# Attention probabilities scaled on GpSimd instead of VectorE, with a ring of factor columns between them

## What is computed

```python
def masked_softmax(s, ok):
    s = jnp.where(ok, s, NEG)
    m = jnp.max(s, -1, keepdims=True)
    e = jnp.where(ok, jnp.exp(s - m), 0.0)
    return e / jnp.maximum(jnp.sum(e, -1, keepdims=True), TINY)
```

```python
    o_att = (gate[..., 0:1] * o_cmp + gate[..., 1:2] * o_slc + gate[..., 2:3] * o_swa).reshape(B, T, D_ATT)
```

## Time and profile before

| | |
|---|---|
| time, median of 3 runs | 2127.87 us (2126.4 to 2128.36) |
| the profiled execution's time | 2130.53 us |
| its span, first to last instruction | 2129.0 us |
| attention, layer 0 | from 204.7 to 394.4 us, 189.7 us |
| attention, layer 1 | from 1102.2 to 1285.8 us, 183.6 us |
| busy share of the span | PE 89%, DVE 53%, ACT 37%, POOL 3% |
| granted TensorE clock, mean of the span | 0.945 of full speed |

### The profile page before, as it was taken

How to read it: one execution, slowest core, us unless ns; L and a number is a source line. 1 busy time by engine, 2 the same in 40 slices (tenths; PEclk the granted TensorE clock), 3 DMA queues, 4 the chain that set the end, 5 groups by cost and what they waited for, 6 DMA issues and landing times.

```text
span 2129.0 us, 25885 instructions
## 1 busy us (share of the span) xinstructions
PE 1901.0 (89%) x9617; PEld 1475.5 (69%) x9617; DVE 1121.8 (53%) x1984; ACT 778.5 (37%) x1110; POOL 69.0 (3%) x80
## 2 busy tenths in 40 slices
PE   6999789979999999989988899749999999999970
PEld 4777555769999999967765558536666666666650
DVE  2684567444544544437746663335555555555546
ACT  3012455332121121130135452345555555555531
POOL 0000000000000000000000000020000000000003
PEclk9999799999999999999999899859999999999995
DMA  6331001011222222053210000158888888888863
GB/s 237 119 96 60 21 20 40 30 50 60 80 80 80 92 85 82 21 168 117 69 60 20 31 30 26 79 202 327 347 345 346 348 346 346 345 347 342 348 276 125
DMA packets 69404, 332.29 MB, mean 156 GB/s; under 512 B 15682, under 2 KB 28802, under 8 KB 50562
## 3 DMA queue, kind: packets, MB, share of 16 engines
q1 hardware_dynamic: 60498, 303.11, 37.9%
q0 software_dynamic: 7088, 24.43, 3.2%
q10 hardware_dynamic: 1728, 3.54, 0.4%
HBM read 312.26 MB, written 22.85 MB: 157 GB/s over the span
## 4 chain that ended last, share of the span: by engine, by line
PE 77%; DVE 9%; DMA 6%; issue 3%; ACT 3%; POOL 1%; SPq 0%; DVEq 0%; ACTq 0%; POOLq 0%
PE ps L1524 24%; PE ps L1317 15%; PE ps L1612 13%; PE ps L1630 7%; DMA w<-in_moe_gu 5%; PE ps L1477 3%; PE ps L1430 3%; PE ps L1459 2%; PE ps L1329 2%; PE ps L1361 2%; DVE w_middle L1237 1%; PE ps L1475 1%; ACT mixed_high L795 1%; DVE parena L852 1%; PE ps L1442 1%
## 5 line engine op out<-in xcount | busy, mean ns | idle before, releaser
L1317 PE MATMUL ps<-h,w 128*128 128x288 f32 x1024 | 253.1, 410 | 15.7 <-ACT h L604 15.7
L1317 PEld LDWEIGHTS ps<-h,w 128*128 128x128 f32 x1024 | 196.4, 192 | 71.6 <-issue 17.1
L1630 PE MATMUL ps<-carena,parena 128*128 128x512 f32 x528 | 237.2, 593 | 0.2 <-DMA carena<-in_moe_dn_last 0.2
L1612 PE MATMUL ps<-mixed_high,hidden_low 128*128 128x512 f32 x576 | 199.4, 417 | 6.3 <-DVE hidden_low L1242 6.3
L685 ACT ACTIVATE w_high<-w 128x1024 fp32r<-128x1024 f32 x82 | 87.0, 1061 | 265.0 <-PE ps L1524 263.8
L795 ACT ACTIVATE mixed_high<-w 128x2048 fp32r<-128x2048 f32 x74 | 137.6, 1907 | 91.1 <-DMA w<-in_moe_gu 88.9
L1612 PE MATMUL ps<-h_high,hidden_low 128*128 128x512 f32 (+1 forms) x576 | 170.6, 374 | 0.0
L1524 PE MATMUL ps<-h_high,w_high 128*128 128x288 f32 x704 | 151.8, 297 | 14.4 <-DVE h_low L1118 14.4
L1630 PEld LDWEIGHTS ps<-carena,parena 128*128 128x128 f32 x528 | 95.2, 190 | 98.7 <-issue 94.1
L1524 PE MATMUL ps<-h_low,w_high 128*128 128x288 f32 x704 | 151.2, 296 | 0.0
L1524 PE MATMUL ps<-h_high,w_low 128*128 128x288 f32 x704 | 151.0, 296 | 0.0
(11 more groups left out here) (305 smaller groups left out, 3189.7 us busy)
## 6 DMA issues: line engine op xcount, KB each, us to landing
w<-in_moe_gu SPq DMA_DIRECT2D x62, 2048.0 KB, 9.1
carena<-in_moe_dn SPq DMA_DIRECT2D x60, 1024.0 KB, 4.9
w<-in_split_w SPq DMA_DIRECT2D x82, 512.0 KB, 3.6
w<-in_w_in SPq DMA_DIRECT2D x8, 2048.0 KB, 10.5
w<-in_moe_gu_last SPq DMA_DIRECT2D x12, 1024.0 KB, 6.7
parena<-sorted_rows POOLq DMA_DIRECT2D x13, 512.0 KB, 8.6
carena<-in_moe_dn_last SPq DMA_DIRECT2D x12, 512.0 KB, 4.8
expert_rows<-parena POOLq DMA_DIRECT2D x12, 512.0 KB, 4.2
```

Of the source, the lines that this page charges most:

```text
L1317: last = M(PS[0:rows, b + n, 0:HALF], w, act_[:, cols], start=(i == 0), stop=(i == len(steps) - 1))
L1612: last = M(PS[:, 2 + c % 2, 0:n], x_[:, k, :], w[:, k, :], start=(k == j == 0), stop=(k == KD - 1 and j == 2))
L1630: last = M(PS[:, 6 + n, :], ehT[:, c % 2, k, :], CA[:, at:at + 512], start=(c == 0 and k == 0), stop=(c == NEC - 1))
```

## The change

The multiplications of `weigh` move from VectorE to GpSimd. VectorE's `factors` writes gate over sum into one of four groups of columns of the tile `sm` (`weight(u, j)`, by u % 4) instead of into `rc`, and reports it by a new semaphore, `p_weight`. GpSimd waits for it, scales the unit's heads one after the other in place, each through `done`, and gives `p_ready` with the last. The compressed branch's small scaling stays on VectorE. The tile `sm` grows from 96 to 112 columns.

```diff
+        def weight(u, j, n=1):
+            return SM[:, 96 + 4 * (u % 4) + j:96 + 4 * (u % 4) + j + n]
@@ GpSimd, in the loop over layers, behind the state's DMAs
+                for u in range(U_L):
+                    kind, i, g, w = units[u]
+                    n = (i + 1) * P if kind == "prompt" else PAST + NS
+                    heads = GRP if kind == "prompt" else 1
+                    pool.wait_ge(p_weight, l * U_L + u + 1)
+                    for j in range(heads):
+                        ins = nc.gpsimd.tensor_scalar(pr[u % 4][:, j, 0:n], pr[u % 4][:, j, 0:n], weight(u, j), None, ALU.mult)
+                        if j == heads - 1:
+                            done(ins, p_ready)
+                        else:
+                            done(ins)
@@ VectorE, sums(u)
-                def factors(sums, gate, n):
+                def factors(out_, sums, gate, n, event=dve_own):
...
-                    done(V.tensor_tensor(rc[:, 0:n], rc[:, 0:n], gate, ALU.mult))
+                    done(V.tensor_tensor(out_, rc[:, 0:n], gate, ALU.mult), event)
...
-                        factors(total(s, 0, GRP), gates[:, :, 1 + w], GRP)
+                        factors(weight(u, 0, GRP), total(s, 0, GRP), gates[:, :, 1 + w], GRP, p_weight)
...
-                        factors(total(s, 0), gs[:, i, 1 + w:2 + w], 1)
+                        factors(weight(u, 0), total(s, 0), gs[:, i, 1 + w:2 + w], 1, p_weight)
@@ VectorE, step u
-                    for j in range(GRP):
-                        if j < to_max:
-                            head_max(u, j)
-                        if j < to_weigh:
-                            weigh(u - 2, j)
+                    for j in range(to_max):
+                        head_max(u, j)
```

More of the change, by code:

```diff
@@ L153, in program @@
         PC = sb("pc", 2 * NBLK)
-        SM = sb("sm", 96)
+        SM = sb("sm", 112)
         BQ = sb("bq", 4 * DEPTH)
@@ L284, in program @@
         conv_done, pooled_ready = (ev(n) for n in ("conv_done", "pooled_ready"))
-        s_full, s_read, p_max, p_exp, p_ready, t_full, t_out, av_done, o_out = (
-            ev(n) for n in ("s_full", "s_read", "p_max", "p_exp", "p_ready", "t_full", "t_out", "av_done", "o_out"))
+        s_full, s_read, p_max, p_exp, p_weight, p_ready, t_full, t_out, av_done, o_out = (
+            ev(n) for n in ("s_full", "s_read", "p_max", "p_exp", "p_weight", "p_ready", "t_full", "t_out", "av_done", "o_out"))
         h_scaled, gate_spread = ev("h_scaled"), ev("gate_spread")
@@ L1040, in sums @@
                             done(V.tensor_reduce(csum, pc3, AX.X, ALU.add))
-                            factors(csum, gates[:, :, 0], GRP)
+                            factors(rc, csum, gates[:, :, 0], GRP)
                             done(V.tensor_tensor(pc3, pc3, rc.unsqueeze(2).to_broadcast([P, GRP, NBP]), ALU.mult))
-                        factors(total(s, 0, GRP), gates[:, :, 1 + w], GRP)
+                        factors(weight(u, 0, GRP), total(s, 0, GRP), gates[:, :, 1 + w], GRP, p_weight)
                     else:
                         if w == 0:
-                            factors(total(s, 4), gs[:, i, 0:1], 1)
+                            factors(rc[:, 0:1], total(s, 4), gs[:, i, 0:1], 1)
                             done(V.tensor_scalar(pc[:, 0:NBLK], pc[:, 0:NBLK], rc[:, 0:1], None, ALU.mult))
-                        factors(total(s, 0), gs[:, i, 1 + w:2 + w], 1)
[L1050 to L1061, removed]
+                        factors(weight(u, 0), total(s, 0), gs[:, i, 1 + w:2 + w], 1, p_weight)
                 def out(u):
@@ L1085, in _ @@
                 for u in range(U_L + 4):
-                    to_max = to_weigh = 0
+                    to_max = 0
                     if u < U_L:
@@ L1091, in _ @@
                         sums(u - 2)
-                        to_weigh = GRP if units[u - 2][0] == "prompt" else 1
-                    for j in range(GRP):
-                        if j < to_max:
-                            head_max(u, j)
-                        if j < to_weigh:
-                            weigh(u - 2, j)
+                    for j in range(to_max):
+                        head_max(u, j)
                     if u >= 4 and u % 2 == 1:
```

## The result

The changed kernel took **2164.4 us** (median of 4 runs, 2161.8 to 2168.1) against 2128.1 for the kernel before beside it. The ratio is 1.0154, with a 95% interval of 1.0133 to 1.0174: slower by 1.5% (the two medians as they stand are 1.7% apart, which the interval takes in), where 2106 and a gain were forecast and the range ended at 2131. The profiled execution has a span of 2166.6 us, 37.6 more than the 2129.0 of before.

The account below looks back on a forecast made before the run. TensorE was taken as busiest in attention, held up by 46.1 us of waits for scaled probabilities. Shorter waits gave 17.1 us, the clock 5, sum 22: from 2130.5 to 2108.5, as median 2106 us; range 2091 to 2131.

Parts of the forecast that it names:

- One scaling on GpSimd: GpSimd's scaling in attention: 0.10 us fixed and 1.17 ns a column, 0.32 to 0.77 us for 128 to 512 columns.
- The break-even: GpSimd's scaling price from which its chain decides and TensorE waits for it: 2.0 ns a column.
- the warning sign: In the changed profile, the sum is wrong if a GpSimd scaling of 512 columns takes over 1.1 us.
- The sum itself: Attention waits: 7.5 us gained a layer, 15.0 in two, with 2.1 for w = 1 units 17.1 us.
- The waits of units with w = 1: TensorE's waits for these units' scaled probabilities, 2.1 us in all, go because their factors come earlier.
- The order of VectorE's queue makes this wait, not the scaling's own length: In attention, TensorE waits because a unit's last scaling stands behind the next unit's last maximum; unit 4: 2.98 us idle.
- The clock: TensorE's granted clock in attention rises 0.01 and a bit more a layer: 5 us gained, between 0 and 12.
- The port: SBUF port shared by VectorE and GpSimd: 0.3 us charged beside sample units; small VectorE instructions stop for 0.3 to 0.8.
- that rival: The maxima share the port too and take turns with GpSimd's scalings: 5 us slower, 2133 us; chance 0.05.
- GpSimd becomes the chain that TensorE waits for: In attention, scalings at the TENSOR_TENSOR's rate make TensorE wait for GpSimd: 2131.6 us; chance 0.07.
- Something else ends last: In attention, TensorE waits instead for ScalarE's copies or the exponentials behind them: 2124 to 2132 us; chance 0.08.
- The ends: First and last units of a layer: unit 0 gains 0.7 us, unit 22 loses 1.1, together -0.4.

Follow-up runs that it names:

- GpSimd's products: The changed kernel, but GpSimd scales each unit with one product of two tensors, the factor column spread over the columns: 2086.7 us, ratio 0.9779.
- the kernel that changes the order alone: The kernel before, scalings kept on VectorE but put straight behind the factors, ahead of the maxima of the unit in front: 2084.8 us, ratio 0.9778.
- the useless products: Extra TensorE products, results unneeded, ahead of waits for scaled probabilities: two in the kernel before, 2107.0 us; three in the changed kernel, 2125.6 us.
- VectorE early: The kernel before, all scalings on VectorE straight behind their factors, ahead of the maxima: 2084.8 us, ratio 0.9778.

## Why the prediction was wrong, point by point

**The failed step is "One scaling on GpSimd".** It placed the price between the MEMSET and the TENSOR_TENSOR by the number of tensors read, "a quarter of the way up, 1.17 ns", with 2.19 as the dear end. Measured: 2.56 ns and 0.28 us fixed in attention, 2.49 and 0.29 alone. The ordering by tensors read has no footing: the copy reads one at 0.84. I had no row of this form and should not have taken the TENSOR_TENSOR as the worst that could come; the bound was as much a guess as the value. The break-even that I gave, 2.0 ns a column, and the warning sign, 512 columns in over 1.1 us, were passed by far (1.59).

**The sum itself holds once it has the right price.** Four heads measure four times L529's mean and three gaps of 0.09: 2.71, 3.98, 5.37 and 6.64 us, which is 1.43, 2.10, 2.89 and 3.56 above my values. Two units of each size in two layers make 4 x 9.98 = 39.9, so the 17.1 us of gain become a loss of 22.8. TensorE's empty time grew by 23.0. So close a fit is in part luck: the sum still holds 2.4 us for the port that were not paid (below), and 0.15 for two hand-overs that took 0.22, 1.1 us in all. The waits of units with w = 1, too, were 3.1 us and not 2.1: I had left out L1459 for tile `x`, 1.0. For GpSimd's products (1.04, 1.89, 2.75 and 3.60) the same working gives a gain of 17.1 - 4 x 0.56 = 14.9; measured 16.0.

**"The order of VectorE's queue makes this wait, not the scaling's own length"** is right, and shown by the kernel that changes the order alone.

**The clock** was mis-sized in its amount, and in its sign for this change. The reading of 2 us for each 0.01 holds roughly: with GpSimd's products layer 0 went from 0.87 to 0.96 and its work from 163.7 to 144.8 us. But I allowed 0.01 and a bit a layer, 5 us in all and 12 at most, where that kernel gained 320.8 - 292.7 = 28.1. I took the clock for a small correction to the waits; in that kernel it gave back more than they did (28.1 against 16.0). In the changed kernel the clock went the other way, 9.0 us lost; there the useless products in the waits got back more than that.

**The port**: the charge of 0.3 beside sample units did not appear. Small VectorE instructions were held now and then, up to 0.51 us, under the 0.8 allowed: of those that ran beside a scaling, 13 of 22 TENSOR_SCALARs on four columns of `sm` (L1020, L1042) and 4 of 16 of L1044; the one-column L1029 never was. In turn GpSimd's scalings were held, but by a larger instruction than the ones I had listed: the four long ones started while VectorE was in L1036, a TENSOR_TENSOR of 1024 columns with two SBUF inputs.

```profile
L1020 DVE TENSOR_SCALAR sm<-sm x32: 169/170/496, 209.3 to 1294.7; 128x4 f32<-128x4 f32 x32
...
L1044 DVE TENSOR_TENSOR sm<-sm,vtok x48: 161/164/512, 213.9 to 1300.9; 128x4 f32<-128x4 f32 x48
```

The maxima kept their durations (0.29 to 0.69 us), so that rival is out. L1028, which reads two operands in `sm`, took its usual time in all 16 cases, in 12 of which one of GpSimd's scalings ran beside it:

```profile
L1028 DVE TENSOR_TENSOR sm<-sm x16: 159/159/160, 215.7 to 1270.6; 128x1 f32<-128x1 f32 x16
```

**The rivals.** "GpSimd becomes the chain that TensorE waits for" named the mechanism, with a chance of 0.07 and a time of 2131.6, since its price stopped at 2.19 ns and it let the clock stay. "Something else ends last" came true only in small, with VectorE early: the 5.6 us behind ScalarE's copies. **The ends**: unit 22 went as signed, but not as sized, its wait rose from 0.23 to 4.53 instead of to 1.3; unit 0 went the other way, from 5.50 to 5.90 where a gain of 0.7 was forecast.

## What to carry to other kernels

A form of instruction that no row shows has no upper bound in the rows of other forms: measure it on the engine before work is moved to it, and if the move loses, try another form of the same operation, or the same order on the old engine, before giving up the idea. Where TensorE's granted clock is below full in a stage in which it waits again and again, compare how long the same work keeps it busy with the waits and without them: a shortened wait can give back more through the clock than by its own length, and a few useless products in the waits show how much that is.

## What the runs showed of the hardware

- **GpSimd's price hangs on the form.** At 512 columns of fp32 a TENSOR_SCALAR takes 1.49 to 1.57 us alone, with a constant or a factor column, in place or not; a TENSOR_TENSOR 1.26, with one side spread from a column 1.04; a COPY 0.62; a MEMSET 0.53. The Trainium skill (GPSIMD Engine Reference, Engine selection) calls one input roughly line rate; the copy agrees, the scaling does not. Why it is the slowest stays open.
- **Who holds VectorE hangs on it too.** Beside GpSimd's TENSOR_TENSOR the same one-column instruction that was never held beside its TENSOR_SCALAR was held 12 times of 13, up to 3.37 us. In this place it waits until GpSimd has ended:

```profile
243.61 1.89 POOL L528 TENSOR_TENSOR x<-x,sm 128x1024 f32<-128x1024 f32 x1 [5.46 <-DVE sm L1040]
...
244.23 1.29 DVE L1024 TENSOR_TENSOR sm<-sm 128x1 f32<-128x1 f32 x1
...
L1024 DVE TENSOR_TENSOR sm<-sm x16: 159/1116/3374, 215.6 to 1199.4; 128x1 f32<-128x1 f32 x16
```

  Both end at 245.5. The Trainium skill (SBUF — State Buffer, Who interferes with whom) says that a VectorE instruction with two SBUF inputs contends with any GpSimd instruction that reads SBUF. GpSimd's TENSOR_TENSOR agrees with it. Its TENSOR_SCALAR, which reads as well, agrees only in part: L1028 was free in 12 of 12 cases and L1044 in 12 of 16, and L1044 went on at most 0.35 us late, with up to 0.86 us of the scaling still to run; but four scalings that began while VectorE's L1036 ran took 0.39 to 0.41 us longer than usual. Why the two forms differ stays open.
- **The clock is part of what waits cost**, shown by the useless products: 2127.4 to 2107.0 us with more work for TensorE, none of it needed.
